# Expert rounds of a hybrid decoder step: single-chunk loads for three more pairs of the last round, and each scatter issued behind the next chunk's products

## The reference, cut to what matters

```
xn = rmsnorm(x, g_ffn)                     # 264 x 2048
# a router picks one of 4 groups, then 2 of its 8 experts, for each token
for g in range(4):                         # 8 experts each, 32 in all
    h = silu(einsum('nd,edf->nef', xn, w_gate[g])) * einsum('nd,edf->nef', xn, w_up[g])
    out = out + einsum('nef,efd->nd', h * combine[:, g, :, None], w_down[g])
y = rmsnorm(x + out, g_final)
```

## Time and profile before

| | us |
|---|---|
| median of 3 runs | 1614.99 (1614.55 to 1615.32) |
| the profiled execution | 1613.94 |
| its span in the trace | 1612.2 |
| PE busy | 1425.0 (88%) |
| DVE busy | 563.2 (35%) |
| ACT busy | 407.5 (25%) |
| mean granted TensorE clock | 0.941 |
| memory read | 540.30 MB |

### The profile page before, as it was taken

How to read it: one execution, slowest core, us unless ns; L and a number is a source line. 1 busy time by engine, 2 the same in 40 slices (tenths; PEclk the granted TensorE clock), 3 DMA queues, 4 the chain that set the end, 5 groups by cost and what they waited for, 6 DMA issues and landing times.

```text
span 1612.2 us, 24095 instructions
## 1 busy us (share of the span) xinstructions
PE 1425.0 (88%) x9915; PEld 935.5 (58%) x9915; DVE 563.2 (35%) x924; ACT 407.5 (25%) x680; POOL 13.6 (1%) x30
## 2 busy tenths in 40 slices
PE   7999999999999999999787778778878878877967
PEld 7999999999999999953232232322322322422421
DVE  5657765554455555542111111111112111111114
ACT  7454344333333344420201101101102002002003
POOL 0000000000000010000000000000000000000000
PEclk9999999999999999999898989889879888889989
DMA  8777445445545659689999999999999999999997
GB/s 331 294 286 262 157 170 182 180 161 196 182 179 179 253 223 351 242 341 429 431 430 428 433 434 425 435 431 429 433 435 430 430 432 429 432 433 432 431 426 298
DMA packets 42364, 544.66 MB, mean 338 GB/s; under 512 B 5809, under 2 KB 5809, under 8 KB 11577
## 3 DMA queue, kind: packets, MB, share of 16 engines
q1 hardware_dynamic: 42178, 544.03, 82.5%
q10 hardware_dynamic: 144, 0.03, 0.0%
HBM read 540.30 MB, written 3.68 MB: 337 GB/s over the span
## 4 chain that ended last, share of the span: by engine, by line
PE 60%; DMA 37%; DVE 1%; ACT 1%; issue 0%; SPq 0%; DVEq 0%; ACTq 0%
DMA ring<-in_expert_chunks 35%; PE bank L1492 12%; PE bank L1493 12%; PE bank L1494 12%; PE bank L1901 5%; PE bank L1898 5%; PE bank L1779 2%; PE bank L1833 2%; DMA ring<-in_dense_units 1%; PE bank L1821 1%; PE bank L1825 1%; PE bank L1814 1%; PE bank L1771 1%; ACT side L909 0%; PE bank L1523 0%
## 5 line engine op out<-in xcount | busy, mean ns | idle before, releaser
L964 DVE TENSOR_TENSOR w_lo<-ring,w_hi 128x1024 fp32r<-128x1024 f32 x220 | 259.9, 1222 | 222.8 <-ACT w_hi L695 222.4
L1492 PE MATMUL bank<-xn_hi,w_hi 128*128 128x264 f32 x1120 | 319.0, 285 | 0.0
L1493 PE MATMUL bank<-xn_lo,w_hi 128*128 128x264 f32 x1120 | 317.3, 283 | 0.0
L1494 PE MATMUL bank<-xn_hi,w_lo 128*128 128x264 f32 x1120 | 317.1, 283 | 0.0
L695 ACT ACTIVATE w_hi<-ring 128x1024 fp32r<-128x1024 f32 x220 | 221.1, 1052 | 366.8 <-PE bank L1494 338.8
L1898 PE MATMUL bank<-side 128*32 128x512 f32 x1024 | 152.3, 736 | 86.6 <-DMA side<-in_expert_chunks 85.0
L1492 PEld LDWEIGHTS bank<-xn_hi,w_hi 128*128 128x128 f32 x1120 | 210.9, 188 | 1.2 <-issue 1.0
L1493 PEld LDWEIGHTS bank<-xn_lo,w_hi 128*128 128x128 f32 x1120 | 211.1, 188 | 0.1
L1494 PEld LDWEIGHTS bank<-xn_hi,w_lo 128*128 128x128 f32 x1120 | 210.0, 187 | 0.0
L1779 PEld LDWEIGHTS bank<-trunk,x_all 128*128 128x128 f32 (+1 forms) x672 | 96.1, 197 | 75.9 <-issue 57.0
L1898 PEld LDWEIGHTS bank<-side 128*32 128x32 f32 x1024 | 33.8, 129 | 181.4 <-DMA side<-in_expert_chunks 101.0
(11 more groups left out here) (308 smaller groups left out, 1648.6 us busy)
## 6 DMA issues: line engine op xcount, KB each, us to landing
ring<-in_expert_chunks SPq DMA_DIRECT2D x34, 4096.0 KB, 33.9
side<-in_expert_chunks SPq DMA_DIRECT2D x28, 4096.0 KB, 38.7
ring<-in_dense_units SPq DMA_DIRECT2D x109, 1024.0 KB, 4.8
trunk<-in_expert_chunks SPq DMA_DIRECT2D x13, 4096.0 KB, 42.9
ring<-in_expert_chunks SPq DMA_DIRECT2D x19, 2048.0 KB, 15.6
ring<-in_expert_chunks SPq DMA_DIRECT2D x18, 1024.0 KB, 19.2
side<-in_expert_chunks SPq DMA_DIRECT2D x8, 2048.0 KB, 10.1
trunk<-in_expert_chunks SPq DMA_DIRECT2D x6, 2048.0 KB, 15.6
```

The source lines that it names most:

```text
L964: V.tensor_tensor(w_lo[n % 2][:, js, :], raw[n % 2][:, js, :], w_hi[n % 2][:, js, :], ALU.subtract).then_inc(lo_done, 1)
L1492: mm(ps[:, 0:n], w_hi[b][:, j, :], x_hi[:, j, :], start=j == k0, stop=False)
L1493: mm(ps[:, 0:n], w_hi[b][:, j, :], x_lo[:, j, :], start=False, stop=False)
L1494: ins = mm(ps[:, 0:n], w_lo[b][:, j, :], x_hi[:, j, :], start=False, stop=j == k1 - 1)
```

## The change

The constant LAST_PAIR goes, and the last round loads pairs 5, 6 and 7 by `ones_after` as well, as single chunks. On PE the line that issues `scatter(0)`, `scatter(1)`, `scatter(2)` ahead of the waits and products of chunks 18, 20 and 22 moves behind these products, in every round.

```diff
-LAST_PAIR = 7
...
-                for q in range(5, LAST_PAIR + 1):
-                    pair_after(q, FREED_BY[q], last, slice(ROUNDS - 1, ROUNDS))
-                for q in range(LAST_PAIR + 1, PAIRS - 1):
+                for q in range(5, PAIRS - 1):
                     ones_after(q, FREED_BY[q], last, slice(ROUNDS - 1, ROUNDS))
...
-                        if c in (18, 20, 22):
-                            scatter((c - 18) // 2)
                         if c == 19:
                             pe.wait_ge(aux_done, it * JPR + (A_E + JOB_LATE + 3))
                             last_columns(0)
...
                         ins.then_inc(e_used, 1)
+                        if c in (18, 20, 22):
+                            scatter((c - 18) // 2)
```

## The result

The changed kernel takes 1616.89 us in the median of 20 runs (1615.51 to 1620.94); the kernel before, run as often beside it, 1613.79 us (1611.68 to 1615.43). The ratio is 1.0021 with a 95% interval from 1.0014 to 1.0027: 2.3 to 4.4 us slower, 3.1 us by the medians. The forecast was +2.5 us, or 1617.5 us for the median. The profiled execution took 1616.33 us against 1613.94 (span 1614.6 against 1612.2), +2.4 us; the prediction had 1616.4 for it.

A forecast was written before the change was run, and what follows sets the result against it. Expert rounds were taken as bound by weight transfers, with PE late at the end. Singles +0.3 and scatter +2.2 make +2.5 us: 1616.4 on the profile's 1613.94, 1617.5 on the median 1614.99; 8-in-10 range 1614.9 to 1619.4.

The forecast's parts named there:

- chunk 16 starts: Last round on PE: with single chunks, chunk 14 starts 4.86 us sooner, so chunk 16 starts at its landing, 1563.8.
- gap ahead of chunk 22: PE idles 2.0 us, from the end of chunk 21 at 1591.3 to chunk 22's landing at 1593.3.
- scatter 2 starts: Ready at 1592.0 but queued behind chunk 22's products, so it starts at 1595.15, where it was at 1592.29.
- last products end: PE's end of the last round: 1601.0 instead of 1599.99, 1.0 us later.
- root on DVE: Final norm: DVE's chain behind scatter 2 becomes the later side; the root starts at about 1605.7, not 1603.20, +2.5 us.
- PE's lateness at chunk 16: Kernel before, last round: PE started chunk 16 4.1 us after its landing, since chunk 14 had to wait for 15.
- The price of the singles: Six more single chunks on SP's queue, 0.05 us each, delay every later landing by 0.3 us; bounds 0 and 6.8 us.
- rival 3: The new DMAs pay their price in series, 6.8 us instead of 0.3: 1624.0 us; chance 0.02.
- Rival 2: Last round: chunk 22's landing follows its issue, 3.8 us sooner, so the end moves by -4.4 us: 1610.6; chance 0.07.
- Rival 4: DVE's chain behind scatter 2 doesn't decide; PE's +1.0 us, or 0.7, is left: 1615.7 to 1616.0; chance 0.11.
- Rival 1: TensorE's clock falls in PE's new gaps, mainly ahead of chunk 22: 1.6 us more (1.2 to 2.4), 1619.1; chance 0.25.
- row of a 1.80 us gap: Evidence against the clock's fall: after a PE wait of 1.80 us the next chunk still took 1.92 us.

The follow-up runs named there:

- e2_scatter: Kernel before with only the scatters moved behind the products of chunks 18, 20 and 22, pairs 5 to 7 left as pairs: 1617.05 us, 1.0020 of the kernel before.
- e4_after_short_gain: Changed kernel without one of DVE's three gain products over the first 1024 columns (sample rows): 1615.93 us, 1.0013 of the kernel before.
- e10_last_behind: The mirror image: changed kernel with scatters 0 and 1 put back ahead of chunks 18 and 20, scatter 2 alone behind: 1617.79 us, 1.0025 of the kernel before.

## Why the prediction was right

By its steps, forecast and measured (profile of the changed kernel):

| step (us) | forecast | measured |
|---|---|---|
| chunk 16 starts | 1563.8 | 1563.85 |
| chunk 17 ends | 1570.8 | 1570.84 |
| chunk 18 starts, at its landing | 1573.6 | 1573.56 |
| gap ahead of chunk 22 | 2.0 | 2.08 |
| chunk 22 starts | 1593.3 | 1593.15 |
| scatter 2 starts | 1595.15 | 1595.00 |
| last products end | 1601.0 | 1600.94 |
| ACT's square root ready | 1604.2 | 1604.10 |
| root on DVE | 1605.7 | 1605.58 |
| the profiled execution | 1616.4 | 1616.33 |

The mechanism was right: in a stage that transfers set, PE has free time ahead of each chunk; the change took scatter 2 out of that time and put it behind the last wait but one. The move removed three stops of 0.7 us that had no more value once PE was at the landings, and the late scatter pushed DVE's chain, which had 0.37 us of slack, by 2.7 us. The two half changes, the mirror image and the kernel with scatter 2 alone put back (0.9994, 1.0020, 1.0025, 1.0005) show that it is this one scatter.

The size was helped by luck in one point. The prediction laid PE's lateness at chunk 16 to the pair alone ("it could start chunk 14 only when 15 was there too"), and took the end of the kernel before as its profile showed it. Part of that lateness was the low clock of chunk 14, which took 3.11 us instead of 1.92, and it reached the end as 0.9 us: 14.3 us from the last landing to the end, against 13.4 in the execution without it. Counted from those 13.4, the changed kernel's 16.6 us are 3.2 more and not the 2.3 that the two profiles show, or the 2.5 of the forecast. How many executions of the kernel before have the one form and how many the other is not known; the 3.1 us of the medians lie between the two.

The price of the singles was right in size, 0.23 us against 0.3. The rule of the Trainium skill that was weighed, a fixed cost of about 2.0 us for each DMA ("DMA: Bandwidth & Descriptors", "Anatomy of one DMA — SWDGE (gpsimd) path"), was fitted to DMAs issued by GpSimd; on SP's full queue no such cost adds up: 0.076 us for each DMA more was measured, so whatever fixed cost there is lies beside the next transfer. That rules out rival 3. Rival 2 is ruled out by chunk 22's landing: issued 3.7 us sooner, landed at the same time. Rival 4 is ruled out by the gain product left out, which shortened DVE's way to the root by its full length.

Rival 1 isn't an alternative but an addition. Its gap (2.0 us) was right, and so was its price of 1.6 us, which the prediction had picked out of 1.2 to 2.4: in the three profiles with the fall at chunk 22, chunk and scatter together took 1.65 us more (e2_scatter 1.14 + 0.51, e4_after_short_gain 1.33 + 0.32, e10_last_behind 0.44 + 1.21). All three are variants; in both profiles of the changed kernel the clock stayed up from chunk 13 of the last round on. That the fall happens there in other executions is likely, since the gap is the same, and not shown. The prediction treated rival 1 as a case for the median, with one chance in four.

The median lies 0.6 us above the changed kernel's profiled execution. The clock could explain this and the long runs, but so could the landings, which moved by 2.4 us in one profile without help of the clock near the end, and the kernel with filled gaps has the same median (1616.92 against 1616.89 and 1616.94 us). No long run of the changed kernel was profiled. What share of the 3.1 us is the clock's stays open.

## What to carry to other kernels

Where an engine waits for transfers, put the work that is ready ahead of the wait, above all in the last round: a stall of 0.7 us for a copy is cheap inside a gap of 2 us, and work moved behind the last waits is paid in full. Before moving work later, follow what hangs behind it on the other engines, and count their slack (here 0.37 us on DVE), as the end may pass to them. Finer loads in a full queue are cheap (0.08 us for each more), but they win only up to the last landing. Compare two profiles by the time behind the last landing, and look for slow products in both, the one before as well, before you read a difference of a microsecond.

## What was not expected of the hardware

Gaps of PE of one length were followed by the 1.2 GHz level in some executions and not in others. Ahead of chunk 22: 2.07 us, and the next eight products took 3.06 instead of 1.92 us; 2.08 us, and they took 3.25; 2.08 us in the changed kernel, and they took 1.92. Ahead of chunk 18: 2.75 us and 3.38, 2.76 us and 1.92. Ahead of chunk 16 much shorter gaps did it: 1.46 us and 3.56, 1.47 us and 3.47, 1.47 us in the changed kernel and 1.92 (ahead of each of these stand 1.0 us of idle time and 0.63 us of transposes). So the prediction's row of a 1.80 us gap without a fall was no sign of safety.

One profile of such a kernel is one draw: the kernel before, profiled at the low clock at chunk 14, looked 0.9 us worse at its end than another execution of its order, and four of the twelve profiles taken after the prediction show a slow chunk 16, 18 or 22 in the last round. The landings are a second draw: the last one moved by up to 3.7 us from profile to profile, and in the latest of them most of it was there in the second of the eight rounds. What sets it in the dense part or the first rounds was not looked into.
